# A diffusion trunk of two layers: pointwise weights by chunk between pairs of modulation units, the first chunk block by block, expert weights in half units

## The chip, the cores and the metric

The kernel runs on one core of one Trainium2 chip. The metric is the device time of one execution in microseconds (us); lower is better. A result is the median of several executions.

## What is computed

One inference step of a trunk with two layers over 640 tokens of width 1024 (512 latent tokens, then 128 context tokens). Each layer has a token mixer and a channel mixer; layer 0 mixes with a Conformer convolution module, layer 1 with a bidirectional state space scan, and both use a mixture of 16 experts behind it. Cut to what the change touches:

```python
# modulation: shift, scale, gate of both sub-layers, from the condition vectors
m = silu(cond) @ ada_w[i] + ada_b[i]            # (1024) @ (1024, 6144)
h = x * (1 + scale) + shift
# Conformer module of layer 0
u = h @ pw1_w + pw1_b                           # (1024, 2048)
a, g = split(u, 2)
u = a * sigmoid(g)
v = depthwise_conv(u, 31 taps along rows of 64) + dw_b
v = silu(layer_norm(v, ln_g, ln_b))
f = v @ pw2_w + pw2_b
x = layer_norm(ALPHA * x + gate * f)
# mixture of experts: each of 16 experts takes the 64 + 16 tokens that score best
hid = silu(xin @ w_gate) * (xin @ w_up)
out = (hid @ w_down) * gates
```

All of it is in float32; the experts' weights are split into a rounded high part and the rest, so that three fast products give nearly float32.

## The kernel before, in words

**Weights.** All large weights come from HBM as a stream `w_stream` of units of 2 MiB (128 partitions x 4096 float32) into a ring of three slots. SP issues them in order of a unit number `u`; `load(u)` waits with `free(u - 3)` until the unit that held the slot is used up, then issues one DMA (L365). Units 0 to 27 hold the modulation weights (`U_ADA`, 12 a layer) and, at 4, 5, 8 and 11, the first pointwise weights (`U_PW1`, two chunks of 128 channels each); 28 and 29 the second pointwise weights; then come six units for each of 16 experts, the scan's units, and the second layer's experts.

**Modulation.** `ada_mm` (L410) multiplies one unit of 512 columns, ACT copies the row (`ada_row`, L912), PE turns it into columns (`ada_tr`, L420), ACT adds the bias into `mT` (`ada_bias`, L921). Units 0 and 1 are shift, 2 and 3 are scale of the first sub-layer, the rest serves later. `gates` (L467) spreads the gate over all partitions, `gate_evac` on ACT (L955) copies it out.

**First stage.** PE runs four modulation units, then `build_hT(0)` (L451) transposes all of X in eight blocks of 128 features, ACT (L949) and DVE (L1385) apply scale and shift into `hT`. `pw1(c)` (L434, L435) multiplies chunk c in two parts (value, gate), each over eight blocks; ACT evacuates with bias (L932 to L936) and sigmoid (L940, L942); DVE multiplies both (`glu`, L313 to L318) and runs 31 taps a chunk (L1430, L1434), in rounds of one, two, two and three chunks (`CONV_DVE`). Modulation units are interleaved between chunks 3 and 7, and the other sixteen run behind chunk 7. Then PE takes the gates, the mean over channels (L518, L519) and, from squares that ACT makes (L1012), the variance (L523, L524); DVE centres and normalises, ACT applies SiLU (L1017), and PE multiplies with the second pointwise weights (L537, L538) into ten tiles, which DVE adds to X (L1391, L1392).

**Experts.** A unit is two halves m of 512 columns over four blocks. For each half ACT rounds the weights to `w_h` (`high`, L1028), DVE takes the rest `w_l` (`low`, L1472), and PE makes twelve products (L552 to L554). The slot is free when `low` of both halves is done. `high` waits for the landing of the whole unit and for the products of four halves before. Between them stand the SiLU (L1034), the gated hidden rows (L1478), their transposes (L560) and split `hidT_h`, `hidT_l` (L1485, L1486). POOL gathers the next expert's rows (L1258) and adds the outputs into HBM (L1267), both by indirect DMAs.

Each engine has one program in the order that the code writes it; a wait stops all that stands behind it on that engine.

Of the kernel before, what the change touches and what calls it, by code (L numbers as in the profile page):

```python
# [44 lines left out]
CONV_DVE = ((0,), (1, 2), (3, 4), (5, 6, 7))  # L45
# [3 lines left out]
U_ADA = (tuple(range(0, 4)) + (6, 7, 9, 10) + tuple(range(12, 16)), tuple(range(16, 28)))  # L49
U_PW1 = (4, 5, 8, 11)  # L50
U_PW2 = 28
U_MOE0 = 30
# [58 lines left out]
def build(nc, w_stream, x_in, params, consts, router, w_dt, ln_rows, pw2_b, ssd_rows, state_in, y_out, state_out,  # L111
          h_rows, z_rows):
    ctx = ExitStack()
    with ctx:
# [166 lines left out]
        landed = [sem(f"slot_landed{i}") for i in range(R)]  # L281
        gathered = [sem(f"gathered{i}") for i in range(2)]
        x_back = [sem(f"x_back{t}") for t in range(NT)]
        o_added = [sem(f"o_added{i}") for i in range(2)]
        names = """wo_high wo_low yT_low lgT_ready logits_tr pool_step csil_zero x_loaded par_loaded cst_loaded wr_loaded ln_loaded pwb_loaded ssdp_loaded state_loaded
# [13 lines left out]

        def gate_part(stage):  # L300
            return 16 if stage % 2 == 0 else 40

        def shift_part(stage):
            return 0 if stage % 2 == 0 else 24

# [22 lines left out]
        def _(sp):  # L328
# [5 lines left out]
            sp.dma_start(X[:, :, :], x_in).then_inc(s["x_loaded"], 16)  # L334

            def used(u):
# [4 lines left out]
                if u in U_PW1:  # L341
                    return s["pw1_done"], 4 * (U_PW1.index(u) + 1)
# [8 lines left out]
            def free(u):  # L351

                for L, u0 in ((0, U_MOE0), (1, U_MOE1)):
                    if u0 <= u < u0 + 6 * EXPERTS:
                        e, k = (u - u0) // 6, (u - u0) % 6
                        low_done(sp, 16 * L + e, 2 * k)
                        low_done(sp, 16 * L + e, 2 * k + 1)
# [14 lines left out]
            for u in range(R, U_SSD + R):  # L372
# [22 lines left out]
        def _(pe):  # L395
            def unit_wait(u0, k):

                j = (u0 + k) % R
                pe.wait_ge(landed[j], 16 * ((u0 + k) // R + 1))
                return ring[j][:, :].rearrange("p (k n) -> p k n", n=512)  # L400

            def ada_mm(L, u):

                w = unit_wait(U_ADA[L][u], 0)
                if 12 * L + u >= 2:
                    pe.wait_ge(s["mrow_ready"], 12 * L + u - 1)
                for r in range(2):
                    for j in range(4):
                        k = 4 * r + j
                        ins = pe.matmul(bank[4 + u % 2][32 * j:32 * j + 32, :], csil[:, k, :], w[:, k, :],  # L410
# [3 lines left out]
            def ada_tr(L, u):  # L414

                pe.wait_ge(s["mrow_ready"], 12 * L + u + 1)
                if 12 * L + u >= 2:
                    pe.wait_ge(s["mT_ready"], 4 * (12 * L + u - 1))
                for i in range(4):
                    ins = pe.matmul(bank[6 + u % 2][:, 2 * i:2 * i + 2], mrow[:, u % 2, i * P:(i + 1) * P], fold,  # L420
                                    start=True, stop=True)
                ins.then_inc(s["ada_tr"], 1)

            def pw1(c):

                for part in range(2):
                    i = 2 * c + part
                    w = unit_wait(U_PW1[c // 2], 0)
                    if i >= 2:
                        pe.wait_ge(s["glu_a"], i - 1)  # L430
                    o = 256 * part + P * (c % 2)
                    for k in range(KC):
                        lw = w[:, k, o:o + P]
                        pe.matmul(bank[i % 2][:, :], lw, hT[:, k, 0:SAMPLE], start=(k == 0), stop=(k == KC - 1))  # L434
                        ins = pe.matmul(bank[2 + i % 2][:, 0:P], lw, hT[:, k, SAMPLE:TOK],  # L435
                                        start=(k == 0), stop=(k == KC - 1))
                    ins.then_inc(s["pw1_done"], 1)

            def build_hT(b, behind=None):

                if b == 0:
                    pe.wait_ge(s["x_loaded"], 16)
                else:
                    pe.wait_ge(s["x_ready"], 5 * b)
# [38 lines left out]
            ada_mm(0, 2)  # L483
            ada_tr(0, 1)
            ada_mm(0, 3)
            ada_tr(0, 2)
            ada_tr(0, 3)
            build_hT(0)
            hT_whole(0)
            for c in range(4):  # L490
                pw1(c)
            ada_mm(0, 4)
            ada_mm(0, 5)
            ada_tr(0, 4)
            pw1(4)
            ada_tr(0, 5)
            pw1(5)
            ada_mm(0, 6)
            ada_mm(0, 7)
            ada_tr(0, 6)  # L500
            pw1(6)
            ada_tr(0, 7)
            pw1(7)
            for u in range(8, 12):
                ada_mm(0, u)
                if u > 8:
                    ada_tr(0, u - 1)
            ada_tr(0, 11)
            for u in range(12):
                ada_mm(1, u)  # L510
                if u:
                    ada_tr(1, u - 1)
            ada_tr(1, 11)
            gates(0)
            pe.wait_ge(s["glu_a"], 16)
            for i, k in enumerate(CONV_ORDER):
# [3 lines left out]
            ins.then_inc(s["mean_mm"], 1)  # L520
# [5 lines left out]
            pe.wait_ge(s["v_ready"], 8)  # L526
# [3 lines left out]
            for nb in range(2):  # L530
                w = unit_wait(U_PW2, nb)
                for t in range(NT):
# [3 lines left out]
                    for k in range(KC):  # L536
                        pe.matmul(bank[i % 8][:, :], v[:, k, t * P:(t + 1) * P], w[:, k, :], start=(k == 0), stop=False)  # L537
# [118 lines left out]
            def ssd_wait(kind, g):  # L656

                u = ssd_unit(kind, g)
                pe.wait_ge(landed[u % R], 16 * (u // R + 1))
# [243 lines left out]
        def _(act):  # L903
# [3 lines left out]
            def ada_row(L, u):  # L907
# [4 lines left out]
                A(mrow[:, u % 2, :], bank[4 + u % 2][:, :], ACT.Copy).then_inc(s["mrow_ready"], 1)  # L912

            def ada_bias(L, u):
# [4 lines left out]
                for i in range(4):  # L919
                    c = 4 * u + i  # L920
                    A(mT[:, L, c, :], bank[6 + u % 2][:, 2 * i:2 * i + 2], ACT.Identity,  # L921
                      bias=ada_bT[:, 48 * L + c:48 * L + c + 1]).then_inc(s["mT_ready"], 1)

            def pw1_evac(c):

                for part in range(2):
                    i = 2 * c + part
                    act.wait_ge(s["pw1_done"], i + 1)
                    a, b = bank[i % 2], bank[2 + i % 2]
# [997 lines left out]
```

## Time and profile before

| | us |
|---|---|
| median of 3 runs | 2455.43 |
| lowest and highest | 2453.04, 2470.23 |
| profiled execution, its own time | 2459.2 |
| its span in the trace | 2457.2 |
| PE, DVE, ACT busy | 2180.2, 1755.5, 1148.3 |

In the profile, PE is TensorE's matmuls, PEld its weight loads, DVE VectorE, ACT ScalarE, POOL GpSimd, SP the engine that issues the weight stream. A row of the timeline begins with its start and its duration; the bracket at its end is the idle time of the engine before it and what ended that. `bank` are PSUM banks, `scr` is the scratch that holds most tiles of a stage, `L12` is line 12 of the kernel. A matmul in float32 shows as two records, so sixteen records are eight products. Busy shares over the whole span are averages over stages with different limits.

### The profile page before, as it was taken

The page shows a single profiled execution, that of the slowest core. Times are in us where ns is not written, and L with a number is a line of the kernel's source. Part 1 is how long each engine was busy: PE and PEld are TensorE (multiplying, and loading weights), DVE is VectorE, ACT ScalarE, POOL GpSimd, SP SyncE. Part 2 cuts the span into 40 slices and gives each one's busy share as a digit, 9 for nine tenths or more (in the row PEclk, how much of TensorE's full clock was granted, in tenths as well). Part 3 has the DMA queues.
Part 4 walks back from the last instruction along what each step waited for, and adds up shares of the span by engine and source line. Part 5 has one row for each costly group of instructions (what it writes and reads, how often), then busy time and mean ns, then how long its engine had stood idle before and what let it go on. Part 6 is the DMA issues. An engine that isn't in the chain of part 4 may idle for free. (4 is left out here: it accounts for less than half of the span.)

```text
span 2457.2 us, 24510 instructions
## 1 busy us (share of the span) xinstructions
PE 2180.2 (89%) x9570; PEld 1351.6 (55%) x9570; DVE 1755.5 (71%) x1889; ACT 1148.3 (47%) x1399; POOL 356.6 (15%) x203
## 2 busy tenths in 40 slices
PE   6998778699999999949899999999759999999992
PEld 3544433466666666635656557466536666666661
DVE  1898733799899889825374653654968898899893
ACT  2112222566666666632512333234236666666672
POOL 1000004111110111040011101101320111110113
PEclk8988889899999999969899999999979999999996
DMA  7145703599999999930023124124249999999992
GB/s 313 73 168 242 340 0 107 194 367 372 362 367 380 356 368 368 359 126 26 26 86 65 35 81 95 52 80 109 78 146 350 359 371 371 362 375 369 372 372 92
DMA packets 51666, 561.18 MB, mean 228 GB/s; under 512 B 6240, under 2 KB 6256, under 8 KB 20448
## 3 DMA queue, kind: packets, MB, share of 16 engines
q1 hardware_dynamic: 37584, 508.80, 53.7%
q0 software_dynamic: 13968, 50.82, 8.1%
q8 instruction: 76, 1.25, 0.2%
q14 instruction: 38, 0.31, 0.0%
HBM read 523.42 MB, written 36.18 MB: 228 GB/s over the span
## 5 line engine op out<-in xcount | busy, mean ns | idle before, releaser
L1472 DVE TENSOR_TENSOR w_l<-ring,w_h 128x2048 fp32r<-128x2048 f32 x384 | 869.8, 2286 | 68.5 <-ACT w_h L1028 66.3
L1028 ACT ACTIVATE w_h<-ring 128x2048 fp32r<-128x2048 f32 x384 | 731.9, 1916 | 324.4 <-PE bank L554 162.9
L552 PE MATMUL bank<-w_h,xin_h 128*80 128x512 f32 x1024 | 407.7, 398 | 3.2 <-DVE xin_l L1492 1.9
L553 PE MATMUL bank<-w_l,xin_h 128*80 128x512 f32 x1024 | 403.1, 394 | 0.0
L554 PE MATMUL bank<-w_h,xin_l 128*80 128x512 f32 x1024 | 400.2, 391 | 0.0
L1267 POOL DMA_INDIRECT z_rows<-hT,slot_i x32 | 101.6, 3174 | 982.0 <-DVE hT L1503 982.0
L552 PE MATMUL bank<-w_h,hidT_h 128*80 128x512 f32 x512 | 206.5, 403 | 36.2 <-DVE hidT_l L1486 36.2
L552 PEld LDWEIGHTS bank<-w_h,xin_h 128*80 128x80 f32 x1024 | 151.9, 148 | 93.9 <-DVE xin_l L1492 11.3
L554 PE MATMUL bank<-w_h,hidT_l 128*80 128x512 f32 x512 | 202.3, 395 | 0.0
L553 PE MATMUL bank<-w_l,hidT_h 128*80 128x512 f32 x512 | 201.7, 394 | 0.0
L554 PEld LDWEIGHTS bank<-w_h,xin_l 128*80 128x80 f32 x1024 | 152.0, 148 | 85.9 <-issue 0.9
L672 PE MATMUL bank<-hT,ring 128*128 128x512 f32 x384 | 198.6, 599 | 0.0
L1434 DVE SCALAR_TENSOR_TENSOR scr<-scr,par 128x640 f32<-128x640 f32 x240 | 193.9, 878 | 1.1
L553 PEld LDWEIGHTS bank<-w_l,xin_h 128*80 128x80 f32 x1024 | 152.1, 149 | 77.0 <-issue 0.7
L708 PE MATMUL bank<-ring,hT 128*128 128x512 f32 x320 | 159.3, 609 | 3.0 <-DVE csT_b L1729 3.0
L434 PE MATMUL bank<-hT,ring 128*128 128x512 f32 x256 | 136.2, 615 | 8.5 <-DMA ring<-w_stream 7.6
L673 PEld LDWEIGHTS bank<-hT,ring 128*128 128x128 f32 x384 | 73.5, 191 | 92.9 <-issue 92.9
L552 PEld LDWEIGHTS bank<-w_h,hidT_h 128*80 128x80 f32 x512 | 76.3, 149 | 86.0 <-DVE hidT_l L1486 51.2
L1231 ACT ACTIVATE scr<-bank,scr 128x128 f32<-128x128 f32 x320 | 88.5, 378 | 34.2 <-PE bank L803 25.0
L1308 POOL TENSOR_TENSOR X<-X,ln_gb 128x1024 f32<-128x1024 f32 x16 | 39.5, 2471 | 437.2 <-ACT X L967 437.2
L554 PEld LDWEIGHTS bank<-w_h,hidT_l 128*80 128x80 f32 x512 | 76.2, 149 | 42.5 <-issue 0.7
L410 PE MATMUL bank<-ring,scr 128*32 128x512 f32 x384 | 63.8, 804 | 38.2 <-DMA ring<-w_stream 38.2
(249 smaller groups left out, 2876.5 us busy)
## 6 DMA issues: line engine op xcount, KB each, us to landing
ring<-w_stream SPq DMA_DIRECT2D x234, 2048.0 KB, 9.9
z_rows<-X POOLq DMA_DIRECT2D x15, 512.0 KB, 8.8
X<-z_rows SPq DMA_DIRECT2D x15, 512.0 KB, 5.3
h_rows<-scr POOLq DMA_DIRECT2D x10, 512.0 KB, 3.9
ln_gb<-ln_rows POOLq DMA_DIRECT2D x4, 1024.0 KB, 6.8
ring<-w_stream SPq DMA_DIRECT2D x4, 1024.0 KB, 5.1
X<-x_in SPq DMA_DIRECT2D x1, 2560.0 KB, 25.8
y_out<-X SPq DMA_DIRECT2D x5, 512.0 KB, 2.6
```

The costliest lines, as they stand in the source:

```text
L434: pe.matmul(bank[i % 2][:, :], lw, hT[:, k, 0:SAMPLE], start=(k == 0), stop=(k == KC - 1))
L552: pe.matmul(out[0:SLOTS, :], ah[:, c, :], wh[:, k, :], start=(first and k == 0), stop=False)
L553: pe.matmul(out[0:SLOTS, :], ah[:, c, :], wl[:, k, :], start=False, stop=False)
L554: ins = pe.matmul(out[0:SLOTS, :], al[:, c, :], wh[:, k, :], start=False, stop=(last and k == 3))
L672: pe.matmul(bank[i % 2][:, :], w[:, k, c0:c0 + P], hT[:, k, 0:SAMPLE], start=(k == 0), stop=(k == KC - 1))
L673: ins = pe.matmul(bank[2 + i % 2][:, 0:P], w[:, k, c0:c0 + P], hT[:, k, SAMPLE:TOK], start=(k == 0), stop=(k == KC - 1))
L708: ins = pe.matmul(bank[(0, 6, 7, 0, 1)[t]][:, :], hT[:, k, t * P:(t + 1) * P], w[:, k, :], start=(k == 0), stop=(k == KC - 1))
L1028: A(w_h[m % NB][:, :, :], src, ACT.Copy).then_inc(s["high_ready"], 1)
L1231: A(Em[:, i % 4, c * P:(c + 1) * P], src, ACT.Exp, bias=lead[:, c, j:j + 1]).then_inc(s["exp_m"], 1)
L1267: pool.indirect_dma_start(z_rows, bass.IndirectOffsetOnAxis(ap=slot_i[0:SLOTS, E % 16:E % 16 + 1], axis=0), out_sb[E % 2][0:SLOTS, :], Non ...
L1434: ins = V.scalar_tensor_tensor(out, shifted(k), dw_w[:, c, k:k + 1], out, ALU.mult, ALU.add)
L1472: V.tensor_tensor(w_l[m % NB][:, :, :], src, w_h[m % NB][:, :, :].bitcast(F32), ALU.subtract)\
```

## The change

- The first pointwise weights come as eight half-size units of 1 MiB, one a chunk. The unit order (`FIRST`) is four modulation units, chunks 0 to 2, five times two modulation units and a chunk, ten modulation units.
- Units 1 and 2 change places (`ADA_COLS`): the first halves of shift and scale come first. X is loaded in two halves of 512 features, the first ahead of unit 2. With that, blocks 0 to 3 are turned and modulated (`first_turn`, `first_evac`) before units 2 and 3 are multiplied, and chunk 0 is made block by block (`first_chunk`).
- From chunk 3 on, a pair of modulation units (`ada_pair`) stands ahead of each chunk, the last ten units behind chunk 7. Four mean parts stand ahead of the last four units, four behind them, and the gates behind the mean.
- DVE's rounds are chunks 0, 1, (2, 3), (4, 5), (6, 7).
- The first tile of the second pointwise product waits for each SiLU by itself.
- In the expert layers each half of a unit has its own DMA, semaphore and release.

```diff
-CONV_DVE = ((0,), (1, 2), (3, 4), (5, 6, 7))
+CONV_DVE = ((0,), (1,), (2, 3), (4, 5), (6, 7))
...
-U_ADA = (tuple(range(0, 4)) + (6, 7, 9, 10) + tuple(range(12, 16)), tuple(range(16, 28)))
-U_PW1 = (4, 5, 8, 11)
+ADA_COLS = ((0, 2, 1, 3) + tuple(range(4, 12)), tuple(range(12)))
+FIRST = (["a"] * 4 + ["p"] * 3 + ["a", "a", "p"] * 5 + ["a"] * 10)
+U_PW1 = [i for i, x in enumerate(FIRST) if x == "p"]
...
+        def ada_bank(L, u):
+            return bank[4 if L == 0 and u in (2, 3) else 4 + u % 2]
...
                 if j == 0:
                     sp.dma_start(cst[:, :], consts).then_inc(s["cst_loaded"], 16)
-            sp.dma_start(X[:, :, :], x_in).then_inc(s["x_loaded"], 16)
+                if j == 1:
+                    sp.dma_start(X[:, :, 0:512], x_in[:, :, 0:512]).then_inc(x_half[0], 16)
...
-                free(u - R)
-                w = UNIT // 2 if U_SSD <= u < U_MOE1 and SSD_UNITS[u - U_SSD][0] == "bc" else UNIT
+                if in_moe(u):
+                    for h in range(2):
+                        free(u - R, (h,))
+                        w = slice(h * HALF, (h + 1) * HALF)
+                        sp.dma_start(ring[j][:, w], w_stream[u, :, w]).then_inc(half_landed[j][h], 16)
+                    return
...
+            def first_turn(k):
+
+                pe.wait_ge(x_half[k // 4], 16)
+                if k >= 2:
+                    pe.wait_ge(s["hTs_ready"], k - 1)
+                for t in range(NT):
+                    if t == NS and k:
+                        pe.wait_ge(s["hTp_ready"], k)
+                    out = bank[(3, 6)[k % 2]][:, t * P:(t + 1) * P] if t < NS else bank[7][:, 0:P]
+                    ins = pe.transpose(out, X[:, t, k * P:(k + 1) * P], ident)
+                ins.then_inc(s["hT_tr"], 1)
+
+            def first_chunk(k):
+
+                w = pw1_in(0)
+                pe.wait_ge(s["hTs_ready"], k + 1)
+                pe.wait_ge(s["hTp_ready"], k + 1)
+                for part in range(2):
+                    lw = w[:, k, P * part:P * (part + 1)]
+                    pe.matmul(bank[part][:, :], lw, hT[:, k, 0:SAMPLE], start=(k == 0), stop=(k == KC - 1))
+                    ins = pe.matmul(bank[(2, 5)[part]][:, 0:P], lw, hT[:, k, SAMPLE:TOK],
+                                    start=(k == 0), stop=(k == KC - 1))
+                    if k == KC - 1:
+                        ins.then_inc(s["pw1_done"], 1)
...
+            def ada_pair(n):
+
+                L, u = n // 12, n % 12
+                ada_mm(L, u)
+                ada_mm(L, u + 1)
+                ada_tr(L, u)
+                ada_tr(L, u + 1)
...
+            pw1(1)
+            pw1(2)
+            ada_done = 4
+            for c in range(3, KC):
+                ada_pair(ada_done)
+                ada_done += 2
+                pw1(c)
+            for u in range(ada_done, 20, 2):
+                ada_pair(u)
...
+            for i in range(4):
+                mean_part(i)
+            ada_pair(20)
+            ada_pair(22)
+            for i in range(4, KC):
+                mean_part(i)
+            gates(0)
...
-            pe.wait_ge(s["v_ready"], 8)
...
+                        if i == 0:
+                            pe.wait_ge(s["v_ready"], k + 1)
...
-                act.wait_ge(landed[j], 16 * ((u0 + 6 * (E % 16) + m // 2) // R + 1))
+                act.wait_ge(half_landed[j][m % 2], halves(u0 + 6 * (E % 16) + m // 2))
```

PE's program at its start, before: `ring` are the weight slots, `cst` the constants with the identity, x8 on L410 is one modulation unit, x4 on L420 its turn, and five transposes on L451 make one block.

```order
L410 MATMUL bank<-ring,scr 32x512 x16
L420 MATMUL bank<-cst,scr 128x2 x4
L410 MATMUL bank<-ring,scr 32x512 x8
L420 MATMUL bank<-cst,scr 128x2 x4
L410 MATMUL bank<-ring,scr 32x512 x8
L420 MATMUL bank<-cst,scr 128x2 x8
L451 MATMUL bank<-cst,X 128x128 x40
L434 MATMUL bank<-hT,ring 128x512
```

And in the changed kernel (L439 is the modulation unit, L447 its turn, L481 a block's transposes, L491 the product of chunk 0):

```order
L439 MATMUL bank<-ring,scr 32x512 x16
L447 MATMUL bank<-cst,scr 128x2 x8
L481 MATMUL bank<-cst,X 128x128 x20
L439 MATMUL bank<-ring,scr 32x512 x8
L447 MATMUL bank<-cst,scr 128x2 x4
L439 MATMUL bank<-ring,scr 32x512 x8
L447 MATMUL bank<-cst,scr 128x2 x4
L491 MATMUL bank<-hT,ring 128x512
L492 MATMUL bank<-hT,ring 128x128
```

Four of the eight blocks have moved ahead of the third and fourth modulation unit, and the products of chunk 0 begin right behind these units, ahead of the other four blocks.

PE's program from the last modulation units to the variance, before (L467 gates, L518 and L519 mean, L523 variance):

```order
L410 MATMUL bank<-ring,scr 32x512 x8
L420 MATMUL bank<-cst,scr 128x2 x8
L467 MATMUL bank<-cst,mT 128x128 x16
L518 MATMUL bank<-scr,cst 128x512
L519 MATMUL bank<-scr,cst 128x128
...
L523 MATMUL bank<-scr,cst 128x512
```

And in the changed kernel, the same stretch (L576 and L577 mean, L439 and L447 the last pairs of units, L530 gates, L591 variance):

```order
L576 MATMUL bank<-scr,cst 128x512
L577 MATMUL bank<-scr,cst 128x128
L439 MATMUL bank<-ring,scr 32x512 x16
L447 MATMUL bank<-cst,scr 128x2 x8
...
L576 MATMUL bank<-scr,cst 128x512
L577 MATMUL bank<-scr,cst 128x128
L530 MATMUL bank<-cst,mT 128x128 x16
L591 MATMUL bank<-scr,cst 128x512
```

The gates have gone behind the mean, of which the last four parts stand behind all modulation units.

SP's program at the first expert layer, before:

```order
L365 DMA ring<-w_stream 128x4096 [waits ada_mm] x16
L365 DMA ring<-w_stream 128x4096 [waits f_mm] x2
L365 DMA ring<-w_stream 128x4096 [waits low_dve] x93
L365 DMA ring<-w_stream 128x2048 [waits low_dve]
L370 DMA X<-z_rows 128x1024 [waits scattered]
```

And in the changed kernel:

```order
L387 DMA ring<-w_stream 128x2048 [waits ada_mm] x2
L387 DMA ring<-w_stream 128x2048 [waits f_mm] x4
L387 DMA ring<-w_stream 128x2048 [waits low_dve] x186
L391 DMA ring<-w_stream 128x2048 [waits low_dve]
L396 DMA X<-z_rows 128x1024 [waits scattered]
```

Twice as many DMAs of half the size, each behind a `low` of its own.

## Rows read from the trace of the kernel before

**Rows 1.** The page: span, and the group of the experts' subtractions.

```profile
span 2457.2 us, 24510 instructions
...
L1472 DVE TENSOR_TENSOR w_l<-ring,w_h 128x2048 fp32r<-128x2048 f32 x384 | 869.8, 2286 | 68.5 <-ACT w_h L1028 66.3
```

**Rows 2.** The timeline of DVE, from the first gating product to the first residual.

```profile
64.91 0.69 DVE L313 TENSOR_TENSOR scr<-scr 128x512 f32<-128x512 f32 x1 [19.15 <-ACT scr L942]
...
66.72 27.59 DVE L1434 SCALAR_TENSOR_TENSOR scr<-scr,par 128x640 f32<-128x640 f32 x30
...
99.60 0.69 DVE L313 TENSOR_TENSOR scr<-scr 128x512 f32<-128x512 f32 x1 [4.26 <-ACT scr L942]
...
101.81 47.84 DVE L1434 SCALAR_TENSOR_TENSOR scr<-scr,par 128x640 f32<-128x640 f32 x60
...
210.59 0.69 DVE L313 TENSOR_TENSOR scr<-scr 128x512 f32<-128x512 f32 x1 [7.48 <-ACT scr L942]
...
213.32 71.72 DVE L1434 SCALAR_TENSOR_TENSOR scr<-scr,par 128x640 f32<-128x640 f32 x90
302.57 0.69 DVE L1443 TENSOR_TENSOR scr<-scr,bank 128x512 f32<-128x512 f32 x1 [17.53 <-PE bank L519]
...
338.75 0.69 DVE L1391 TENSOR_TENSOR tmp<-bank,gate_bc 128x512 f32<-128x512 f32 x1 [13.32 <-PE bank L538]
```

**Rows 3.** The timeline of PE and ACT, from the second modulation unit to chunk 1.

```profile
21.63 0.60 ACT L912 ACTIVATE scr<-bank 128x512 f32<-128x512 f32 x1 [7.88 <-PE bank L410]
...
33.81 3.30 PE L410 MATMUL bank<-ring,scr 128*32 128x512 f32 x16 [6.10 <-DMA ring<-w_stream]
...
42.24 1.44 PE L451 MATMUL bank<-cst,X 128*128 128x128 f32 x10 [0.20 <-ACT hT L949]
...
56.48 1.28 ACT L940 ACT_TABLE_LOAD   x1
...
72.45 0.69 ACT L932 ACTIVATE scr<-bank,par 128x512 f32<-128x512 f32 x1 [7.57 <-PE bank L435]
...
81.10 0.69 ACT L940 ACTIVATE scr<-bank,par 128x512 f32<-128x512 f32 x1 [7.39 <-PE bank L435]
```

**Rows 4.** The timelines of PE and ACT, from the gates to the first tile.

```profile
288.34 5.47 PE L467 MATMUL bank<-cst,mT 128*128 128x128 f32 x32 [0.81 <-ACT mT L921]
...
303.61 0.74 ACT L1012 ACTIVATE scr<-scr 128x640 f32<-128x640 f32 x1 [9.17 <-DVE scr L1445]
...
320.74 6.60 ACT L1017 ACTIVATE scr<-scr,par 128x640 f32<-128x640 f32 x8
...
327.39 10.20 PE L537 MATMUL bank<-ring,scr 128*128 128x512 f32 x16 [13.86 <-ACT scr L1017]
```

**Rows 5.** The waits over twelve experts of layer 0: total us, times, longest.

```profile
ACT w_h L1028 <- DMA ring<-w_stream: 68.5, 36, 3.6
...
PE bank L552 <- DVE hidT_l L1486: 16.4, 12, 2.6
```

**Rows 6.** Stretches, the first two of twelve experts each: busy time, PEclk, DMA share, GB/s.

```profile
548.80:981.30 432.50, 416.06 (x1921) 267.60 (x1920) 386.52 (x265) 292.37 (x193) 67.65 (x25) 1.00 0.99 368
1919.10:2349.30 430.20, 414.92 (x1921) 266.75 (x1920) 386.20 (x265) 292.32 (x193) 67.68 (x25) 1.00 0.99 370
...
735.00:743.00 8.00, 8.00 (x40) 5.21 (x39) 6.57 (x6) 5.67 (x4) 0.00 (x0) 1.00 1.02 337
745.00:752.00 7.00, 6.71 (x35) 4.25 (x33) 6.11 (x5) 5.73 (x4) 0.00 (x0) 1.00 1.01 431
753.00:754.00 1.00, 1.00 (x6) 0.67 (x5) 1.00 (x2) 1.00 (x1) 0.00 (x0) 1.00 0.82 246
```

**Rows 7.** Issue to landing, us: 1 MiB units and gathers (page), one unit alone at 81.1.

```profile
ring<-w_stream SPq DMA_DIRECT2D x4, 1024.0 KB, 5.1
...
scr<-h_rows,slot_i POOLq DMA_INDIRECT x32, 13.2
...
DMA to landing us min/median/max: 7.6/7.6/7.6
```

More of the change, by code:

```diff
@@ L304, in shift_part, with in_moe, whole, halves @@
             return 0 if stage % 2 == 0 else 24
+        def in_moe(u):
+            return U_MOE0 <= u < U_SSD or u >= U_MOE1
+        def whole(u):
+            return 16 * len([i for i in range(u % R, u + 1, R) if not in_moe(i)])
+        def halves(u):
+            return 16 * len([i for i in range(u % R, u + 1, R) if in_moe(i)])
         def low_done(eng, E, m):
@@ L370, in x_reload @@
                     sp.dma_start(X[:, t, :], z_rows[t * P:(t + 1) * P, :]).then_inc(x_back[t], 16)
-            for u in range(R, U_SSD + R):
+            for u in range(R, U_PW1[0] + 1):
+                load(u)
+            sp.dma_start(X[:, :, 512:D], x_in[:, :, 512:D]).then_inc(x_half[1], 16)
+            for u in range(U_PW1[0] + 1, U_SSD + R):
                 load(u)
@@ L482, in _, with mean_part @@
             ada_tr(0, 0)
-            ada_mm(0, 2)
             ada_tr(0, 1)
[L485 to L490, printed above, removed]
-                pw1(c)
[L492 to L516, printed above, removed]
+            for k in range(4):
+                first_turn(k)
+            for u in (2, 3):
+                ada_mm(0, u)
+                ada_tr(0, u)
+            pe.wait_ge(s["mT_ready"], 8)
+            for k in range(4):
+                first_chunk(k)
+            first_turn(4)
+            first_turn(5)
+            for k in range(4, 6):
+                first_chunk(k)
+                first_turn(k + 2)
+            first_chunk(6)
+            first_chunk(7)
+            pw1(1)
[4 more added lines that the diff above has]
+                ada_done += 2
+                pw1(c)
+            for u in range(ada_done, 20, 2):
+                ada_pair(u)
+            def mean_part(i):
+                k = CONV_ORDER[i]
                 pe.wait_ge(s["conv_ready"], i + 1)
@@ L911, in ada_row @@
                     act.wait_ge(s["ada_tr"], 12 * L + u - 1)
[L912 removed]
+                A(mrow[:, u % 2, :], ada_bank(L, u)[:, :], ACT.Copy).then_inc(s["mrow_ready"], 1)
             def ada_bias(L, u):
@@ L950, in hT_evac, with first_evac @@
                       scale=mT[:, L, sh + 8 + k, 0:1]).then_inc(s["hTs_ready"], 1)
+            def first_evac(k):
+                act.wait_ge(s["mT_ready"], 8 if k < 4 else 16)
+                act.wait_ge(s["hT_tr"], k + 1)
+                A(hT[:, k, 0:SAMPLE], bank[(3, 6)[k % 2]][:, :], ACT.Identity, bias=mT[:, 0, k, 0:1],
+                  scale=mT[:, 0, 8 + k, 0:1]).then_inc(s["hTs_ready"], 1)
             def gate_evac(b, b0=4):
@@ L1420, in _ @@
                                     1.0, None, ALU.add).then_inc(s["adab_ready"], 1)
-            hT_evac(0)
+            for k in range(KC):
+                first_evac(k)
             for chunks in CONV_DVE:
```

132 lines of the change are left out of this document (70 added, 62 removed).

## The prediction

> **What bounds the kernel now.** I read the page first: a span of 2457.2 us [rows 1], in an execution of 2459.2 us. That is 3.8 us above the median of 2455.43; I work the change out against the profiled execution and take the same number of microseconds off the median. Then I read the timeline by engine, since the kernel has stages with different limits, and the edits lie in two of them.
>
> The first stage, up to the products with the second pointwise weights, hangs on DVE. Its taps run from 66.72 to 285.0 with hardly a break [rows 2], because one tap over 640 columns takes 0.8 to 0.9 us and there are 31 for each of 8 channel chunks. Look for the four gaps that end at 64.91, 99.60, 210.59 and 302.57: in the first three DVE waits for ACT's evacuation of a pointwise chunk, in the last for the mean. The mean was late for a reason that DVE's rows do not show: PE takes the gates at 288.34 [rows 4], behind the last modulation unit, and the means of eight chunks after them.
>
> The mixtures of experts take about half of the time. Over 12 experts of layer 0 PE is busy 416.06 of 432.50 us, and over 12 of layer 1 414.92 of 430.20 [rows 6]. So PE idles 16.4 and 15.3 us, 1.32 us an expert, and the waits name one cause: PE waits 16.4 us in 12 times for `hidT_l` from DVE, while ACT waits 68.5 us in 36 times for a landing of `ring` [rows 5]. One wait feeds the other: a late landing delays ACT's `w_h` (L1028), DVE's `w_l` (L1472) behind it, and in DVE's queue the `hidT_l` of the second hidden half.
>
> **Start of the taps.** ACT's copy of the second modulation unit starts at 21.63 [rows 3], and both units are now the first halves of shift and scale. With transposes and bias (some 3.5 us) the first four blocks can be turned from about 24.5 on, at 0.82 us a block (two in 1.63 us, as `build_hT` does them at L451), and PE is free near 27.5. Two more units follow, each 3.3 us [rows 3] and about 2.5 us for copy, turn and bias, one behind the other because both use bank 4: PE reaches the first block of chunk 0 at 38.9. The data is there: a 2 MiB unit passes in 4.9 us at the 431 GB/s of a full stream [rows 6], so the half of X, two units and the half-size unit behind the landing near 17.9 are in by 33.5. Chunk 0 is 17.3 us of matmuls (one part ends 8.65 us after another: 72.45 and 81.10 in [rows 3]); with four turns of 0.65 and a short wait it ends at 59.1. Both parts now end together, so the three copies (some 1.3 us; the first has 0.69 at 72.45) and the table load (1.28 us at 56.48) that stood beside the second part come behind it: 3.1 us in all, DVE starts at 62.2 instead of 64.91: **2.7 us gained**. Bounds: at 57 if PE's clock is high from 28 us on (modulation units of 3.3 us would take 1.9), at 66 if chunk 0's first blocks run at the low clock. The lines of 2 KB in X's halves have no row; between the full stream rate and a third of it they cost 0 to 5 us, and I take nothing, since the second half has 9 us to spare.
>
> **The taps.** Chunk 1 gets a round of its own. Alone, 30 taps take 27.59 us, in a pair 47.84 / 2 = 23.9 [rows 2]: 3.7 us lost. The gaps of 4.26 and 7.48 us and a small one (0.2) close if the chunks arrive in time. After chunk 0 PE needs 17.3 us a chunk, and from chunk 3 on a pair of modulation units of some 5.8 us ahead of each. From 59.1 that gives chunk 3 at 117, chunk 5 at 163, chunk 7 at 209. DVE asks for them at 62.2 + 58.6 = 121, 172 and 223. Each half-size unit is asked for when its slot comes free and lands in 5.1 us [rows 7] beside the pair's 5.8, so it is hidden, by less than 1 us; if not, chunk 3 has 4 us to spare. Net **8.2 us gained**; taps end at 274.1 instead of 285.0. Bounds 4 to 8.2, since chunks 3 and 5 could still be late.
>
> **Mean, gates, variance.** After chunk 7 ten modulation units remain, limited by the stream at 4.9 us; they end near 256, 18 us before the taps. So when the last chunk is done only two mean parts are left: 2.1 us each at the low clock, which PE has after idling from 256. DVE's wait of 17.53 becomes 3.7: **13.8 us gained**. In exchange the gates, once ahead of the mean, now stand behind it on PE (5.3 us from 288.34 to the mean, partly at a low clock [rows 4]) and their copies stand ahead of the squares (L1012) in ACT's queue. Squares start about 5.4 us after DVE's first centred chunk where it was 1.0 us: **4.4 us lost**. Bounds 3 and 6.
>
> **First tile.** PE waited for all eight SiLUs (6.60 us from 320.74) and took 10.20 us over the first eight matmuls from 327.39 [rows 4]. Now it follows them one by one. It cannot use all of that overlap, but it starts seven SiLUs of 0.83 us earlier at the same low clock: **5.8 us gained**. At a higher clock it would be bound by the SiLUs and gain no less. Everything behind the first tile, at 338.75 [rows 2], moves with it, since the next tiles are PE's alone. Stage: 2.7 + 8.2 + 13.8 - 4.4 + 5.8 = 26 us, bounds 16 to 33.
>
> **Half units of the experts.** SP waited for both halves of a unit, then sent 2 MiB; now the first half goes when its own subtraction is done, one subtraction of 2.29 us [rows 1] or more earlier, and ACT starts on the first half when 1 MiB has landed, 2.5 us earlier (7.6 alone against 5.1 for 1 MiB [rows 7]). Together that is nearly 5 us against ACT's worst wait of 3.6 us [rows 5]. The 16 DMA engines are 99% busy [rows 6], which speaks against any gain; but busy is not fast: around 753, where a unit was asked for too late, they moved 246 GB/s, while from 745 to 752 they moved 431. Earlier requests fill such dips. Of PE's 1.32 us an expert I leave 0.35 and take 28 of 32 experts (the first and last of a layer idle little): 28 x 0.97 = 27, rounded to **26 us**. Bounds 0 and 32 (all of PE's idle time in the two windows).
>
> The Trainium skill's page DMA: Bandwidth & Descriptors says, in its section Anatomy of one DMA, that a DMA has a fixed cost of about 2 us besides its bytes, and under Rules for kernel authors that small transfers should be joined, with 1 MiB or more for full rate. The half units sit just on that line. The trace agrees on the fixed part (5.1 us for 1 MiB, where 2.5 us are bytes) and also shows that it passes beside another transfer (431 GB/s over 7 us). By the rule alone the gain would be lost, which is the third rival.
>
> Sum: 26 + 26 = 52 us, 2407 for the profiled execution, 2403.5 on the median; I say 2405.
>
> **The rivals.**
> - The DMA engines are really full. Gathers and scatters take their share (337 GB/s from 735 to 743 [rows 6]), and earlier requests only queue longer. For it: the 99%; against it: the dip at 753. Then only the first stage gains: 2455 - 26 = 2429. Chance 0.17.
> - The first stage gains less: low clock in chunk 0 and late chunks leave 16 us, the experts 26: 2413. For it: the margin under 1 us. Chance 0.11.
> - Slower: the dips belong to each start of a transfer, not to a late request. A dip costs about 0.5 us; six more starts an expert cost 3 us, and with engines at 99% this becomes the period of 32 experts: 96 us, less 26: about 2525. It decides from 0.8 us an expert on. Against it: the full rate from 745 to 752 holds across a unit's end. Chance 0.04.
> - The gather of the next expert's rows comes too late. It takes 13.2 us in the middle [rows 7] beside one or two units; a fuller queue could stretch it past the moment PE turns the rows, and PE's idle time would only change its name: 2429 again. Chance 0.03. The same page, under Queues, rings and completion order, says that each DMA engine takes queues in turn; by that a fuller queue costs the gather at most its turns, and no run here shows it.
>
> **How the numbers follow.** The forecast has 0.65. A measurement tells about 1% (24.6 us) from no change. The forecast and the second rival are faster by more than that; of the two cases at 2429 (0.20), which straddle the border at 2431, half counts as faster and half as same: faster 0.86, same 0.10, slower 0.04. The range runs from 2388 (33 + 32 us, and a little for the median's spread) to 2437 (first stage alone, at 18 us).
>
> **What would show it.** Right: DVE's first gating product near 62 and no gap above 1 us between taps; mean wait under 5 us; squares of ACT behind gate copies; first residual product near 312; expert period near 34.9 us, ACT's waits for `ring` well below 68.5 us in 12 experts and PE busy above 98% of such a window. Wrong: PE still waiting for `hidT_l` as before with DMA at 99%; rates under 368 GB/s with half units; a wait for the gathered rows on PE.

## The result, and the profile after

The changed kernel takes 2392.89 us (median of 4 runs, 2392.21 to 2395.72) where the kernel before, beside it, takes 2454.23 (2448.36 to 2470.23). The ratio is 0.9742, with an interval of 0.9696 to 0.9789: 52 to 75 us less. The forecast of 2405 comes from a sum of 52 us; the medians lie 61 us apart. So the sign is right, the measured time lies in the stated range of 2388 to 2437, and the size was forecast a little low.

The profiled execution of the changed kernel took 2395.72 us, its span 2393.9; against [rows 1] that is 63.3 us less. The ledger below uses one more run: the kernel before was profiled a second time (its experiment is the last one below). Each entry is the start of one instruction, in us:

| | before | before, again | after |
|---|---|---|---|
| first residual product of the first stage | 338.75 | 340.64 | 310.69 |
| first SiLU of layer 0's experts | 478.36 | 480.09 | 454.75 |
| last SiLU of layer 0's experts | 1028.12 | 1029.31 | 986.07 |
| first subtraction of layer 1's experts | 1830.51 | 1822.42 | 1778.64 |
| first SiLU of layer 1's experts | 1846.90 | 1839.84 | 1800.21 |
| last SiLU of layer 1's experts | 2395.02 | 2391.93 | 2331.29 |
| end | 2457.23 | 2453.93 | 2393.9 |

Between the first and the last column the first stage gives 28.1 us. The experts give 18.4 and 17.0 us between their first and last SiLU, but lose 4.5 us ahead of layer 0's first SiLU and 5.2 us ahead of layer 1's: net 25.8. The scan between the layers gives 9.8 us, the tail behind the last SiLU loses 0.4. The sum is 63.3. Against the second trace of the kernel before, the same entries give 29.9 for the first stage, 30.2 net for the experts, 0.5 for the scan and -0.6 for the tail, 60.0 in all. So a stage's gain is known to a few microseconds only, and the scan's 9.8 are no gain of the change.

**First stage.** The timeline of DVE in the changed kernel, to be held against [rows 2] (start, duration, and in brackets the idle time before and what ended it):

```profile
60.81 0.69 DVE L332 TENSOR_TENSOR scr<-scr 128x512 f32<-128x512 f32 x1 [6.52 <-ACT scr L1013]
...
62.61 27.59 DVE L1516 SCALAR_TENSOR_TENSOR scr<-scr,par 128x640 f32<-128x640 f32 x30
...
91.91 27.59 DVE L1516 SCALAR_TENSOR_TENSOR scr<-scr,par 128x640 f32<-128x640 f32 x30
...
122.77 47.84 DVE L1516 SCALAR_TENSOR_TENSOR scr<-scr,par 128x640 f32<-128x640 f32 x60
...
224.99 47.83 DVE L1516 SCALAR_TENSOR_TENSOR scr<-scr,par 128x640 f32<-128x640 f32 x60
276.82 0.69 DVE L1525 TENSOR_TENSOR scr<-scr,bank 128x512 f32<-128x512 f32 x1 [4.00 <-PE bank L577]
...
297.29 5.97 DVE L1536 TENSOR_TENSOR scr<-scr 128x640 f32<-128x640 f32 x8 [0.80 <-ACT scr L1088]
310.69 0.69 DVE L1472 TENSOR_TENSOR tmp<-bank,gate_bc 128x512 f32<-128x512 f32 x1 [7.42 <-PE bank L607]
```

Look at the brackets: between 60.81 and the end of the taps at 272.82 none is left. The gaps of 4.26 and 7.48 us have gone, the wait for the mean is 4.00 instead of 17.53, and the wait for the first tile 7.42 instead of 13.32.

**Experts.** The same windows as in [rows 6], twelve periods of each layer (PE, PEld, DVE, ACT and POOL busy, PEclk, DMA share, GB/s):

```profile
524.00:940.30 416.30, 414.40 (x1921) 266.91 (x1920) 384.79 (x265) 295.68 (x192) 67.48 (x25) 1.00 1.01 382
1869.20:2285.60 416.40, 414.50 (x1922) 266.92 (x1921) 385.18 (x265) 295.70 (x193) 67.32 (x25) 1.00 1.01 382
```

PE idles 1.9 us in twelve experts, where it idled 16.4 and 15.3. The period, one expert's time, is 34.70 us from the second expert on: PE's own work and 0.16 us of idle time. The same bytes pass in less time, at 382 instead of 368 GB/s, with a DMA share that says "full" in both (1.01 and 0.99). The waits of twelve experts (total us, times, longest) show what has gone from [rows 5]:

```profile
ACT w_h L1102 <- PE bank L623: 102.3, 120, 1.2
...
PE bank L621 <- DVE hidT_l L1568: 1.9, 12, 0.2
```

No row of ACT waiting for `ring` is left in that stretch; ACT now waits for PE, which is what a kernel bound by PE looks like. On the page, the units are halves:

```profile
L1554 DVE TENSOR_TENSOR w_l<-ring,w_h 128x2048 fp32r<-128x2048 f32 x384 | 869.4, 2285 | 38.4 <-ACT w_h L1102 36.0
...
ring<-w_stream SPq DMA_DIRECT2D x396, 1024.0 KB, 8.1
ring<-w_stream SPq DMA_DIRECT2D x38, 2048.0 KB, 9.5
```

**What was given back.** Ahead of the first expert of a layer PE waits for the first gathered rows. The timelines of POOL (first line), SP's queue (second) and PE (third) around that place in the changed kernel:

```profile
433.90 2.88 POOL L1332 DMA_INDIRECT scr<-h_rows,slot_i  x1 [13.83 <-DVE scr L1657]
...
435.97 12.38 SPq L387 DMA_DIRECT2D ring<-w_stream  x3
...
443.46 1.33 PE L639 MATMUL bank<-cst,scr 80*128 80x80 f32 x8 [10.13 <-DMA scr<-h_rows,slot_i]
...
446.53 0.63 PE L622 MATMUL bank<-w_l,xin_h 128*80 128x512 f32 x1
```

And in the kernel before:

```profile
462.12 2.88 POOL L1258 DMA_INDIRECT scr<-h_rows,slot_i  x1 [13.83 <-DVE scr L1575]
...
466.45 8.88 SPq L365 DMA_DIRECT2D ring<-w_stream  x2
...
468.20 1.33 PE L570 MATMUL bank<-cst,scr 80*128 80x80 f32 x8 [6.66 <-DMA scr<-h_rows,slot_i]
```

The gather is the same. Before, SP's first load of a freed slot starts 4.3 us behind the gather's issue and the rows are there after 6.0 us. Now a half is free after one subtraction, the load starts 2.1 us behind, and the rows take 9.5 us. In layer 1 the rows take 5.8 against 10.0 us.

### The profile page after: what moved, and what is told of

It reads as the page before. It is cut to its first block and busy times, and to the rows that moved or that the text cites. A ratio compares the mean times of both kernels' runs of the same rounds, so it can differ in the third digit from the quotient of the medians.

```text
span 2393.9 us, 24513 instructions
## 1 busy us (share of the span) xinstructions
PE 2158.0 (90%) x9570; PEld 1344.2 (56%) x9570; DVE 1755.1 (73%) x1889; ACT 1157.3 (48%) x1399; POOL 355.2 (15%) x203
## 5 line engine op out<-in xcount | busy, mean ns | idle before, releaser
L621 PEld LDWEIGHTS bank<-w_h,xin_h 128*80 128x80 f32 x1024 | 152.3, 149 | 93.3 <-DVE xin_l L1574 10.4
L741 PE MATMUL bank<-hT,ring 128*128 128x512 f32 x384 | 196.8, 594 | 0.0
L467 PE MATMUL bank<-hT,ring 128*128 128x512 f32 x224 | 115.2, 596 | 0.4 <-ACT scr L1007 0.4
L622 PEld LDWEIGHTS bank<-w_l,hidT_h 128*80 128x80 f32 x512 | 76.1, 149 | 34.1
```

The costliest lines, as they stand in the source:

```text
L621: pe.matmul(out[0:SLOTS, :], ah[:, c, :], wh[:, k, :], start=(first and k == 0), stop=False)
L622: pe.matmul(out[0:SLOTS, :], ah[:, c, :], wl[:, k, :], start=False, stop=False)
L741: pe.matmul(bank[i % 2][:, :], w[:, k, c0:c0 + P], hT[:, k, 0:SAMPLE], start=(k == 0), stop=(k == KC - 1))
```

## The experiments

Each kernel ran beside the kernel before; ratios are to that. "Period sum" is the time from the first SiLU of the first expert to that of the sixteenth, 15 periods, for layer 0 and layer 1 (before 537.6 and 537.1, in its second trace 537.8 and 541.1; after 520.3 and 520.0). All such sums and marks are read from one profiled execution of each kernel.

**Do the two gains add up?** The changed kernel with whole units for the experts:

```diff
         def in_moe(u):
-            return U_MOE0 <= u < U_SSD or u >= U_MOE1
+            return False
...
-                act.wait_ge(half_landed[j][m % 2], halves(u0 + 6 * (E % 16) + m // 2))
+                act.wait_ge(landed[j], whole(u0 + 6 * (E % 16) + m // 2))
```

> The changed kernel with the expert layers' loads put back: whole units of 2 MiB, one semaphore, one release. My theory (two gains that add up): the first stage keeps its 28 us (first residual product near 310.7), the expert period goes back to about 35.8 us with about 1.3 us of PE idle in each, the first gather of a layer is quick again (6 us): about 2454 - 28 = 2426 us. Rival (the experts run better only because they start at another time): the period stays near 34.7 us and the time near 2395.

Measured 2432.11 us, ratio 0.9899 (0.9865 to 0.9932). The first residual product stands at 312.50, the period sums are 534.8 and 541.5, and the first gathers take 6.0 and 5.9 us.

The kernel before with the half units alone (the change's lines for the experts' loads put into it):

> The kernel before with half units in the expert layers and nothing else of the change. My theory: expert period 34.7 us and PE idle 0.16 in each, that is 17 us less a layer, less 4 us a layer that the first gather loses beside the early loads: 2454 - 26 = 2428 us, first residual product unchanged at 338.8. Rival (the DMA engines were full, the gain needs the new first stage): period 35.5 or more, 2445 to 2454.

Measured 2425.63 us, ratio 0.9872 (0.9832 to 0.9913); residual at 342.46, period sums 520.1 and 520.1, first gathers 9.5 and 9.7 us. Each part does its share alone, the halves with their loss at the first gathers too. 1.0% and 1.3% make up nearly all of 2.6%.

**Is it the earlier request?** Both halves are asked for only when the whole slot is free:

```diff
-                        free(u - R, (h,))
+                        free(u - R, (0, 1))
```

> The changed kernel, but both halves of an expert unit are asked for only when the whole slot is free; each half still has its own DMA and its own landing. It tells an early request from an early landing and from shorter lines (8 KB). My theory (the early request fills the dips of the stream): the dips return, ACT waits for ring again, period 35.0 to 35.6 us: 2403 to 2421. First rival (the first half's landing alone is what counts) or second rival (8 KB lines let gathers through sooner): period 34.7 to 34.8 us, about 2393.

Measured 2385.81 us, ratio 0.9729 (0.9686 to 0.9772). The period sums are 520.2 and 520.3. The waits of twelve experts:

```profile
ACT w_h L1102 <- DMA ring<-w_stream: 11.2, 14, 1.3
...
PE bank L621 <- DVE hidT_l L1568: 1.9, 12, 0.2
```

ACT waits a little for landings again, but never over 1.3 us, and PE does not notice. So the earlier request, on which the forecast put the gain, earns nothing in the periods as long as ACT starts on the first half. The trace shows what it costs: without it the first gathers take 6.0 and 5.9 us, and layer 0's first SiLU comes at 449.46 instead of 454.75. Of these 5.3 us, 1.5 stand already at the first residual product (309.20 against 310.69), which the edit does not touch; 3.8 belong to the gather.

**Is it the earlier use?** Early requests, but ACT starts on either half when both have landed:

```diff
-                act.wait_ge(half_landed[j][m % 2], halves(u0 + 6 * (E % 16) + m // 2))
+                for h in range(2):
+                    act.wait_ge(half_landed[j][h], halves(u0 + 6 * (E % 16) + m // 2))
```

> The changed kernel, but ACT starts on either half only when both halves of the unit have landed; requests stay early. My theory (early request): the stream stays full, period at most 35.0 us, 2393 to 2402. Rival (early landing): ACT waits for the second half as before, period near 35.5 us, about 2420.

Measured 2399.09 us, ratio 0.9767 (0.9727 to 0.9807). Most periods are 34.73 us, a few 35.6; sums 523.6 and 522.1. ACT waits longer, PE hardly:

```profile
ACT w_h L1103 <- DMA ring<-w_stream: 35.6, 23, 3.1
...
PE bank L621 <- DVE hidT_l L1569: 2.9, 12, 1.1
```

That left two readings: each of the two is enough, or neither matters and it is the shape, two transfers with lines of 8 KB in place of one with 16 KB. So both edits went in together:

> The changed kernel, still with two transfers of 1 MiB for a unit of an expert, but both asked for only when the whole slot is free, and ACT starts on either half only when both have landed; so only the shape of the transfers is left of the half units. Theory one (two transfers with lines of 8 KB beat one with lines of 16 KB beside the gathers and scatters, whatever the time of asking and of use): the period stays 34.7 us, PE idles under 0.5 us an expert, the first gathers of a layer take 6 us, 2386 to 2392 us. Theory two (asking early and starting early are each enough alone to cover the wait, and the last two kernels each kept one of them): the period goes back to 35.6 to 35.8 us with PE waiting for hidT_l, 16 us a layer, as with whole units: 2424 to 2432 us.

Measured 2412.30 us, ratio 0.9813 (0.9783 to 0.9843). The period sums are 531.5 and 527.8 us:

```profile
ACT w_h L1103 <- DMA ring<-w_stream: 63.1, 35, 3.4
...
PEld bank L621 <- DVE hidT_l L1569: 16.2, 12, 2.1
...
PE bank L621 <- DVE hidT_l L1569: 10.6, 12, 1.6
```

The wait is back: ACT's nearly as in [rows 5], PE's for two thirds. So the second theory holds in kind, but the time lies between the two bands: the periods are 35.4 and 35.2, not 35.6 or more. Over both layers the sums read 1076.3 with whole units, 1059.2 with halves late in both ways, 1045.7 with early requests alone, 1040.5 with early use alone, 1040.3 with both. So some 17 us come with the shape, a further 14 or 19 with one of the two timings, and hardly anything is left for the other. The shape's share is the least certain: the sums of one layer with whole units spread from 534.8 to 541.5 us over three traces, and there is one trace with halves late in both ways. How the shape helps (shorter lines, or two starts) was not told apart.

**What do the first gathers cost?** SP holds the first reload of a layer until the first gather has landed:

```diff
                 if in_moe(u):
+                    if u in (U_MOE0 + R, U_MOE1 + R):
+                        sp.wait_ge(gathered[0], 16 * (1 if u < U_SSD else 9))
```

> The changed kernel; in each expert layer SP holds its first reload back until the first expert's gathered rows have landed. Theory (the early half loads slow that gather from 6 to 9.5 us, and PE waits for it): the first gather takes about 6 us again, the first expert starts 3.5 to 4.5 us earlier in each layer, 7 to 9 us in all: about 2385. Rival (the loads held back are then late themselves): PE waits in the first expert instead, 2391 to 2396.

Measured 2385.42 us, ratio 0.9734 (0.9699 to 0.9770). POOL and PE at the first gather:

```profile
429.66 2.88 POOL L1334 DMA_INDIRECT scr<-h_rows,slot_i  x1 [12.43 <-DVE scr L1659]
...
435.75 1.33 PE L641 MATMUL bank<-cst,scr 80*128 80x80 f32 x8 [6.65 <-DMA scr<-h_rows,slot_i]
```

The gathers take 6.0 and 5.8 us and the periods stay (520.2 and 520.4). The medians are 7.5 us apart, but each stands beside its own runs of the kernel before, and the two ratios (0.9734 and 0.9742) hardly differ; so the gain rests on the trace. There the way from the first residual product to layer 0's first SiLU takes 140.3 us instead of 144.1, and the way from layer 1's first subtraction to its first SiLU 17.4 instead of 21.6: 8.0 us in all. The first residual product itself comes 4.0 us earlier (306.74), in a stage that the edit does not touch; that is spread.

**The place of the gates.** They go ahead of the last four mean parts:

```diff
+            gates(0)
             for i in range(4, KC):
                 mean_part(i)
-            gates(0)
```

> The changed kernel with the gates ahead of the last four mean parts instead of behind them. Theory (the gates stand in the way of ACT's squares, as the prediction's term of 4.4 us says): first square within 1.2 us of the first centred chunk, variance 4 to 5 us earlier, about 2388.5. Rival (the gates warm PE's clock for the variance, or PE's own pace bounds that stretch): less than 1.5 us gained, 2391 to 2394.

Measured 2393.26 us, ratio 0.9755 (0.9715 to 0.9794): nothing that the medians show. In the trace the first square stands 1.04 us behind the first centred chunk (277.43 on ACT, 276.39 on DVE) instead of 4.64 (281.46 and 276.82). But PE does the first products of the variance slower: 11.57 us pass from the first square to the variance on DVE (289.00) instead of 9.94. In both kernels PE has idled ahead of the last mean parts (7.17 and 10.41 us) and does them at a low clock; in the changed kernel the gates then stand between them and the variance. The windows of the first variance products (columns as above), here and in the changed kernel:

```profile
278.20:281.90 3.70, 3.68 (x9) 2.03 (x10) 3.56 (x9) 1.47 (x2) 0.00 (x0) 0.61 0.00 0
...
282.20:286.00 3.80, 3.76 (x13) 2.18 (x14) 1.99 (x5) 2.17 (x4) 0.00 (x0) 1.00 0.00 0
```

The granted clock is 0.61 against 1.00. Of 3.6 us, 2.4 arrive at the first residual (308.32 against 310.69).

**The first tile.** PE waits for all eight SiLUs again:

```diff
                         if i == 0:
-                            pe.wait_ge(s["v_ready"], k + 1)
+                            pe.wait_ge(s["v_ready"], 8)
```

> The changed kernel, with the first tile of the second pointwise product waiting for all eight SiLUs as before. Theory: the 5.8 us of overlap are lost, about 2399. Rival (the clock, low after the longer idle time, eats it either way): 2 us or less, 2393 to 2395.

Measured 2400.32 us, ratio 0.9783 (0.9749 to 0.9817). From the variance on DVE to the first residual 23.83 us pass instead of 19.29 (291.40 to 310.69). PE's row here:

```profile
305.43 8.76 PE L606 MATMUL bank<-ring,scr 128*128 128x512 f32 x16 [13.95 <-ACT scr L1091]
```

Its first matmul comes 5.7 us later behind the variance than in the changed kernel, but the eight products take 8.76 instead of 9.88 us, since none waits for a SiLU any more; together 4.5 us at the first residual.

**DVE's rounds.** The changed kernel with the rounds of before:

```diff
-CONV_DVE = ((0,), (1,), (2, 3), (4, 5), (6, 7))
+CONV_DVE = ((0,), (1, 2), (3, 4), (5, 6, 7))
```

> The changed kernel with DVE's rounds of before: chunks 0, (1, 2), (3, 4), (5, 6, 7), and the means in that order. Theory: the 3.7 us of a lone chunk come back as a gain, but DVE now waits for chunk 2 (ready near 95 where it is asked for near 90: 4.5 us lost) and the gap at the last round of three opens by some 2 us; the sum is a loss of 2 to 5 us: 2395 to 2398. Rival (the rounds of before were simply cheaper): 3 us gained, 2390.

Measured 2406.32 us, ratio 0.9805 (0.9773 to 0.9838); the taps end at 285.67 instead of 272.82, a miss of the expectation. DVE's timeline names the places:

```profile
94.70 0.69 DVE L332 TENSOR_TENSOR scr<-scr 128x512 f32<-128x512 f32 x1 [3.37 <-ACT scr L1013]
...
211.22 0.69 DVE L332 TENSOR_TENSOR scr<-scr 128x512 f32<-128x512 f32 x1 [13.19 <-ACT scr L1013]
```

Chunk 2 is 3.37 us late for the second round, and chunk 7 13.19 us for a last round of three, which asks for it at 198; 16.6 us of gaps less the 3.7 that a pair saves are the 12.9. So with the old rounds PE's new order brings the taps nothing: they end at 285.67, and at 285.0 in the kernel before [rows 2]. The first residual product still comes 16.0 us earlier than there (322.75 against 338.75), by what changed behind the taps. The new rounds with the old order were not run.

**The best of them together.** The held reload with the early gates:

> The changed kernel with two moves: SP holds the first reload of an expert layer until the first gather has landed, and PE takes the gates ahead of the last four mean parts. Expected 7 us from the first (two gathers back from 9.5 and 10 to 6 us) and 1 to 2.4 us from the second: 2382 to 2386 us; if the gates' place is worth nothing, as its median alone said, 2385 to 2386 us.

The late request with the early gates:

> The changed kernel with both halves of an expert's unit asked for only when the whole slot is free, and the gates ahead of the last four mean parts. Expected 7 us from the first (first gathers of 6 us, period unchanged at 34.7 us) and 1 to 2.4 us from the second: 2382 to 2386 us, the same as the version that holds the reload within 2 us; if asking early is worth something in the periods that the profile of one execution did not show, it is slower than that version.

Measured 2388.23 us, ratio 0.9702 (0.9674 to 0.9730), and 2388.52 us, ratio 0.9713 (0.9689 to 0.9738). The medians miss the expectation by 2 us; the kernel before stood at 2462.28 beside them, and the two ratios are the lowest of all, but their intervals overlap with that of the changed kernel (0.9696 to 0.9789). In the traces layer 0's first SiLU comes at 445.59 and 442.31 instead of 454.75, of which 4.4 and 7.8 us stand at the first residual product already, and the scan took 8.5 us longer than after the change (801.2 and 801.0 against 792.6). Either is a version to keep; that it beats the changed kernel rests on the traces of the edited places.

**Whose are the 10 us in the scan?** The kernel before, unchanged, profiled again:

> The kernel before once more, unchanged, for a second profiled execution of it. The two traces differ by 11 us in the scan stage too (814.5 against 803.6 us from the last SiLU of layer 0's experts to the first subtraction of layer 1's), where no line was edited. Theory one (the longer scan belongs to that one execution): the second execution of the kernel before takes 803 to 807 us there. Theory two (it belongs to the kernel before, by what its experts leave behind): 812 to 816 us again. The first residual product near 338.8 us and 15 periods of 537 us in both cases, and a ratio of 1.

Measured 2453.76 us, a ratio of 1.0006 (0.9985 to 1.0026). From the first SiLU of the last expert to layer 1's first subtraction it took 804.5 us (the marks from which the 814.5 and 803.6 us of the expectation were taken), so theory one holds. Windows of the scan (columns as above), the first execution of the kernel before:

```profile
1028.10:1200.00 171.90, 130.92 (x616) 90.41 (x614) 67.71 (x115) 55.36 (x106) 31.91 (x23) 0.81 0.27 95
...
1600.00:1830.50 230.50, 191.46 (x827) 126.84 (x825) 150.03 (x268) 83.19 (x181) 46.75 (x35) 0.93 0.30 96
```

The second execution:

```profile
1029.30:1201.20 171.90, 130.61 (x656) 88.74 (x655) 72.35 (x121) 60.13 (x125) 31.91 (x23) 0.85 0.27 95
...
1601.20:1822.40 221.20, 183.88 (x793) 123.68 (x791) 141.66 (x251) 81.78 (x177) 46.74 (x35) 0.92 0.30 93
```

In the first 171.9 us the granted clock was 0.81 instead of 0.85, and PE got through 616 matmuls instead of 656 in the same busy time; the last stretch had to make up for them. So the scan's clock differs between executions of one kernel, by 9 us of its time. The other traces bear it out: from the last SiLU of layer 0 to layer 1's first subtraction the scan took 792.3 to 795.5 us in eleven of the fourteen traces of this case and 801.0 to 802.4 in three, and no edit changed what it computes. Why the clock differs is not shown.

## Why the prediction was right, and where its reason was wrong

- **Start of the taps.** The forecast was 62.2, the trace has 60.81. PE took the first product of chunk 0 at 37.70 (forecast 38.9) and ran at the high clock from there; three copies and the table load came behind it as counted. PE waited for neither half of X. So 4.1 us are gained instead of 2.7; but the start itself moves between executions, from 64.91 to 68.39 in the three traces with the old first stage and from 58.59 to 62.72 in the eleven with the new one, so the two sizes can't be told apart.
- **The taps.** Their end was forecast at 274.1 and measured at 272.82, all of the 1.3 us from the earlier start: 8.1 of the 8.2 us came, and no chunk was late.
- **Mean, gates, variance.** DVE's wait for the mean is 4.00 us (forecast 3.7), so 13.5 are gained. The squares start 4.64 us behind the first centred chunk (forecast 5.4), and from that chunk to the variance on DVE 14.58 us pass instead of 11.0: 3.6 lost (forecast 4.4). Moving the gates back gains 2.4, not 3.6, since with the gates behind the mean it is they, and not the variance, that PE does while its clock comes up (0.84 from 276.50 to 281.00, 1.00 from 282.20 on).
- **First tile.** It gained 5.9 us by the traces (25.18 against 19.29 us up to the first residual), 4.5 by the edit alone; the forecast was 5.8. The stage is 28.1 us (29.9 against the second trace of the kernel before), forecast 26.
- **Half units.** In sum 25.8 us net (30.2 against the second trace of the kernel before), forecast 26; that the first pair agrees so well is luck, for a gain that was put too low met a loss that was not foreseen. The step that did not hold is "Earlier requests fill such dips" as the reason of the gain. Asked for late, the halves gave the same period. What decides is that ACT's waits for `ring` shrink, and earlier request or earlier start does that alone: ACT waits 35.6 or 11.2 us in twelve experts, against 63.1 with neither, and PE 2.9 or 1.9. So the prediction's "nearly 5 us" of both together is more than was needed, and it had no term for the shape of the transfers, with which nearly half of the gain in the periods comes (17 of 36 us). It then kept 0.35 us of idle time an expert and left out four experts (and took its product of 27 as 26), whereas PE kept 0.16 and the 30 periods gained 34.4 us together, or 38.6 against the second trace.
- **Not foreseen.** The earlier request has a victim. The fourth rival asked whether the gather of the *next* expert would come too late. From a layer's fourth expert on that gather took 10.4 to 12.9 us after the change, where the median before is 13.2 [rows 7], so the fuller queue did not stretch it; and it landed 38 us or more before PE turned its rows (26 for the second expert, and 19 or more before the change), so this rival was never near. The first gather of a layer has no time to spare, and lost 3.5 and 4.2 us; with PE at its low clock behind it that came to 9.6 us in all. The Trainium skill's page DMA: Bandwidth & Descriptors, under Rules for kernel authors, advises issuing a DMA early and waiting for it late, so that its fixed part overlaps. Here early issue alone did cover most of the wait (1045.7 against 1059.2 us over the 30 periods); but beside the earlier start it added nothing there (1040.3 against 1040.5), and where another transfer was the one waited for it cost 9.6 us.
- **The rivals.** The full DMA engines: refuted, since the same bytes passed at 382 GB/s instead of 368 with a share of 1.01 against 0.99. A first stage of only 16 us: refuted by the 28.1. A price for each start that makes the kernel slower: refuted, twice the transfers ran at a higher rate. Measured, the whole units are 36 us slower over the 30 periods. The prediction read the rule of the Trainium skill's same section, to join small transfers, as speaking against the halves; but that rule asks for 1 MiB or more, which a half unit has, so it was no reason for this rival. The 2 us of fixed cost that the prediction took from the same page stand there, in Anatomy of one DMA, for DMAs that GpSimd issues; SP issues this ring, and its trace shows 2.6 us (5.1 less 2.5).
- **The 9 us above the forecast** are not settled to the microsecond. By the first trace of the kernel before, 2 lie in the first stage and the rest in the scan; by the second, 4 lie in the first stage and 4 in the experts. The two traces differ by 9.3 us in the scan alone, so this is spread that the forecast could not have named.

## What to carry to other kernels

Where a ring's landing is late by a few microseconds in a cycle, split the transfer and either ask or start by halves; test each alone, because the two cover the same wait, and asking late may spare another transfer. When loads move ahead, look for the small transfer at a stage's start that nothing covers, and let it pass first. Before a stage that no edit touched is given a share of the gain, profile the old kernel a second time. A DMA share near 1 does not say that the stream is full (0.99 stood beside 368 GB/s here, 1.01 beside 382): compare GB/s of the same bytes.

## What the hardware showed that was not expected

- A gather that takes 6.0 us with its first 4.3 us alone takes 9.5 and 10.0 us when a 1 MiB load starts 2.1 us behind it. The Trainium skill's page DMA: Bandwidth & Descriptors says in Queues, rings and completion order that a DMA engine goes round its queues packet by packet; the trace fits that: in layer 0 the gather landed at 443.42, later than alone, but while a second 1 MiB load (issued at 438.17, landed at 448.31) was still under way.
- PE comes out of the wait for the first gather at the low clock (1.2 GHz). Two windows of the changed kernel, behind its first transposes:

```profile
443.40:449.20 5.80, 4.48 (x16) 3.04 (x17) 4.39 (x4) 2.67 (x3) 0.89 (x1) 0.50 0.78 210
449.20:455.00 5.80, 5.80 (x21) 3.57 (x20) 2.52 (x2) 3.45 (x3) 0.00 (x0) 0.76 0.89 340
```

The same two of the kernel before (columns as above):

```profile
468.20:474.00 5.80, 4.54 (x17) 3.11 (x18) 4.45 (x4) 2.67 (x3) 0.90 (x1) 0.54 0.96 351
474.00:479.80 5.80, 5.80 (x27) 3.73 (x26) 3.22 (x2) 4.65 (x4) 0.00 (x0) 1.00 0.97 302
```

Both start at half clock, with 0.63 us a matmul; in the kernel before, the second window is at full clock (2.4 GHz), in the changed one not yet (0.76), and PE gets through 21 matmuls instead of 27. Ahead of these windows PE idled for 10.13 us in the changed kernel and for 6.66 before. So 4.5 us are lost at this place while the gather itself took 3.5 longer.
